# A streaming encoder step: the FFN up projection as seven block products for 768 of 1088 token columns

## The reference

```python
h = h + concat([conv_out, ret_out]) @ w_out
f = square(relu(rmsnorm(h, norm_ffn_w) @ w_up)) @ w_down     # w_up (1024, 4096), w_down (4096, 1024)
y = rmsnorm(h + f, norm_final_w)                             # 1024 prompt rows, 64 sample rows
```

## Time and profile before

| | |
|---|---|
| median of 3 runs | 1220.26 us (1220.0 to 1220.28) |
| profiled execution, first to last instruction (span) | 1218.5 us |
| granted TensorE clock | 1.000 of full speed, whole span |
| a middle group, up half | 23.76 us |
| the same group, down half | 20.90 us |

### The profile page before, as it was taken

One profiled execution on the slowest core, in us unless ns is written; L12 is line 12 of the kernel. 1 busy time (PEld: TensorE's weight loads), 2 busy tenths in 40 slices (PEclk: granted clock), 3 DMA queues, 4 the chain that ended last, 5 costly groups with the idle time before them and its releaser, 6 DMA issues.

```text
span 1218.5 us, 20456 instructions
## 1 busy us (share of the span) xinstructions
PE 1209.5 (99%) x6671; PEld 1119.4 (92%) x6671; DVE 763.3 (63%) x1483; ACT 524.4 (43%) x1154; POOL 290.9 (24%) x228
## 2 busy tenths in 40 slices
PE   8999999999999999999999999999999999999998
PEld 6899999999999888989989988998998998998996
DVE  5345665665666363477577568568568567666747
ACT  6414324333244342435434534544544533543546
POOL 0000000000000000252452452453353344345213
PEclk9999999999999999999999999999999999999999
DMA  7011111111111530121011111202201202102104
GB/s 265 22 35 40 40 46 37 48 37 37 51 42 63 180 106 1 52 70 61 25 53 60 46 31 60 67 10 60 69 9 60 69 9 69 60 9 69 52 18 148
DMA packets 84990, 69.52 MB, mean 57 GB/s; under 512 B 9416, under 2 KB 68816, under 8 KB 84960
## 3 DMA queue, kind: packets, MB, share of 16 engines
q1 hardware_dynamic: 84816, 68.89, 18.4%
q10 hardware_dynamic: 144, 0.26, 0.1%
HBM read 64.14 MB, written 4.99 MB: 57 GB/s over the span
## 4 chain that ended last, share of the span: by engine, by line
PE 98%; DMA 0%; ACT 0%; DVE 0%; SPq 0%; issue 0%; DVEq 0%; ACTq 0%
PE pp L1533 30%; PE pp L1535 30%; PE pp L1534 30%; PE pp L1539 1%; PE pp L1540 1%; PE pp L1730 1%; PE pp L1659 1%; PE pp L1670 1%; PE pp L1652 1%; PE pp L1669 1%; PE pp L1550 0%; DMA xr<-in_x_prompt 0%; PE pp L1641 0%; PE pp L1676 0%; SPq L474 0%; ACT junk L619 0%
## 5 line engine op out<-in xcount | busy, mean ns | idle before, releaser
L1535 PE MATMUL pp<-mid_hi,ws_lo 128*128 128x368 f32 (+1 forms) x768 | 251.4, 327 | 0.0
L1533 PE MATMUL pp<-mid_hi,ws_hi 128*128 128x368 f32 (+1 forms) x768 | 251.1, 327 | 0.0
L1534 PE MATMUL pp<-mid_lo,ws_hi 128*128 128x368 f32 (+1 forms) x768 | 250.8, 327 | 0.0
L1533 PE MATMUL pp<-hn_hi,ws_hi 128*128 128x368 f32 (+2 forms) x576 | 191.8, 333 | 0.0
L1341 DVE TENSOR_TENSOR h<-pp,h 128x512 f32<-128x512 f32 x300 | 190.3, 676 | 0.0
L1481 POOL TENSOR_TENSOR h<-tmp,h 128x512 f32<-128x512 f32 x120 | 158.4, 1352 | 131.6 <-ACT tmp L844 131.6
L1534 PE MATMUL pp<-hn_lo,ws_hi 128*128 128x368 f32 (+2 forms) x576 | 188.9, 328 | 0.0
L1535 PE MATMUL pp<-hn_hi,ws_lo 128*128 128x368 f32 (+2 forms) x576 | 188.8, 328 | 0.0
L1533 PE MATMUL pp<-do_hi,fo_hi 128*128 128x512 f32 x452 | 176.0, 389 | 0.0
L1534 PE MATMUL pp<-do_lo,fo_hi 128*128 128x512 f32 x452 | 175.9, 389 | 0.0
L1535 PE MATMUL pp<-do_hi,fo_lo 128*128 128x512 f32 x452 | 175.9, 389 | 0.0
(11 more groups left out here) (214 smaller groups left out, 1901.5 us busy)
## 6 DMA issues: line engine op xcount, KB each, us to landing
raw<-in_w_up SPq DMA_DIRECT2D x64, 256.0 KB, 4.8
dr<-in_w_down SPq DMA_DIRECT2D x64, 256.0 KB, 3.5
raw<-in_w_in SPq DMA_DIRECT2D x48, 256.0 KB, 2.9
xr<-in_x_prompt SPq DMA_DIRECT2D x8, 512.0 KB, 6.1
raw<-in_w_out SPq DMA_DIRECT2D x16, 256.0 KB, 3.3
out<-hw SPq DMA_DIRECT2D x9, 256.0 KB, 2.0
wv_raw<-in_w_in SPq DMA_DIRECT2D x8, 256.0 KB, 5.9
h<-in_x_prompt SPq DMA_DIRECT2D x2, 1024.0 KB, 7.9
```

Of the source, the lines that this page charges most:

```text
L1533: pe.matmul(out, a_hi, b_hi, start=start, stop=False, skip_group_check=again)
L1534: pe.matmul(out, a_hi, b_lo, start=False, stop=False, skip_group_check=again)
L1535: return pe.matmul(out, a_lo, b_hi, start=False, stop=stop, skip_group_check=again)
```

## The change

The up projection of token columns 0 to 767 becomes seven products as well. With the `w_up` slice of a group as four blocks A11, A12 (`a` = 0, contraction halves 0 and 1), A21, A22 (`a` = 1) and the tokens as blocks B11, B21 (columns 0 to 383) and B12, B22 (384 to 767):
- GpSimd combines the weights in each group: S3 = A11 - A21, S2 = A22 - S3, S4 = A12 - S2, S1 = A21 + A22.
- The combinations of the normed tokens (T1 to T4) are made once, by GpSimd beside the output projection, written to a device memory tensor `xt_dram` and read back; T1 goes over columns 384 to 767 of `mid`'s first contraction half, where B12 stood. B22 stays in the second half.
- TensorE's up half of groups 1 to 15 is D0, P1, P2, P6, P5, P7, P3, P4, D1. D0 and D1 are the direct products of the remaining 320 columns (256 prompt, 64 sample). P6, P7, P4 accumulate on P1 in bank 1; P3 on P5 in bank 2. Three intermediate results are copied out by ScalarE (`tap_copy`) for VectorE's sums (`c_sum`) before the bank goes on. Group 0 keeps the direct form for all columns (`up_first`), with parts of 384, 384 and 320.
- Weights, activations and their combinations share nine slots (`A_AT`, `W_AT`), and most raw data stands in place where its lo part is then written; `tmp`, `raw`, `dr` and the small sample tiles of the feed-forward part have no region of their own any more.
- The sample rows' relu and square move from ScalarE to VectorE (`sample_relu`). Their products move from the end of the down half to a place behind P1, into banks 4 and 5, which P2's third and fourth quarter use next.
- `OUT_TILES` becomes 0, 3, 1, 4, 8, 2, 5, 6, 7, and the pieces of `h` are waited for accordingly.

The core of the diff:

```diff
-CGY = [(0, 368), (368, 368), (736, 352)]
+SB = 384
+CGY = [(0, SB), (SB, SB), (2 * SB, TY - 2 * SB)]
+DIRECT = 2 * SB
...
+A_AT = {"A11": 0, "A21": 1, "A12": 2, "A22": 3, "S3": 4, "S2": 5, "S1": 6, "S4": 1}
+W_AT = {"A11": 0, "A12": 2, "S1": 3, "S3": 4, "S2": 5, "S4": 6, "A21": 7, "A22": 8}
+UPS = ["D0", "P1", "P2", "P6", "P5", "P7", "P3", "P4", "D1"]
+UP_BANK = {"D0": 0, "P1": 1, "P6": 1, "P7": 1, "P4": 1, "P2": 2, "P5": 2, "P3": 2, "D1": 3}
-ORDER = [*[(p, q) for p in range(OPS) for q in range(QUADS)], "sample"]
+ORDER = [*[(P1, q) for q in range(QUADS)], ("sample", 0), ("sample", 1), *[(p, q) for p in range(P2, OPS) for q in range(QUADS)]]
...
# ScalarE
+            def up_group(g):
+                w_hi_part(g, "S2")
+                w_hi_part(g, "S1")
+                f_direct(g, 0)
+                f_hi(g, "f1", F_HI)
+                d_hi_next(g, "B11")
+                tap_copy(g, "P1")
+                w_hi_part(g, "S3")
+                d_hi_next(g, "T1")
+                f_added(g, "C11")
+                w_hi_part(g, "S4")
+                tap_copy(g, "P6")
+                d_hi_next(g, "B21")
+                w_hi_part(g, "A22")
+                tap_copy(g, "P5")
+                d_hi_next(g, "T3")
+                w_hi_part(g, "A21")
+                f_added(g, "C22")
+                d_hi_next(g, "B22")
+                f_added(g, "C12")
+                f_hi(g, "A11", F_HI)
+                d_hi_next(g, "T2")
+                f_c21(g)
+                f_hi(g, "A12", F_HI)
+                d_hi_next(g, "T4")
+                f_direct(g, 1)
...
# VectorE
+            def up_group(g):
+                w_lo_part(g, "S2")
+                w_lo_part(g, "S1")
+                sample_relu(g, 0)
+                w_lo_part(g, "S3")
+                c_sum(g, "C11")
+                w_lo_part(g, "S4")
+                d_low(g, "B11", D_LO, D_HI)
+                d_low(g, "T1", D_LO, D_HI)
+                w_lo_part(g, "A22")
+                c_sum(g, "C22")
+                w_lo_part(g, "A21")
+                d_low(g, "B22", D_LO, D_HI)
+                c_sum(g, "C12")
+                d_low(g, "B21", D_LO, D_HI)
+                d_low(g, "T2", D_LO, D_HI)
+                d_low(g, "T3", D_LO, D_HI)
                 f_low(g, "A11", F_HI)
...
+                d_low(g, "T4", D_LO, D_HI)
+                f_low(g, "A12", F_HI)
+                sample_relu(g, 1)
+
+            def down_group(g, first):
+                dve.wait_ge(s_relu, 2 * g + 2)
+                dve.tensor_tensor(sf_raw(2), sf_raw(0), sf_raw(1), ALU.add).then_inc(f_sum_dve, 1)
+                dve.wait_ge(f_sum_dve, 3 * g + 1)
                 f_low(g, "f1", F_HI)
...
+                dve.tensor_tensor(fo_raw[:, A_AT["S2"], :], fr[:, 1, 512:1024], fo_raw[:, A_AT["S3"], :], ALU.add).then_inc(f_sum_dve, 1)
+                f_low(g, "f2", F_HI)
+                f_low(g, "f12", F_HI)
+                dve.tensor_tensor(fo_raw[:, A_AT["S1"], :], fr[:, 0, 512:1024], fr[:, 1, 512:1024], ALU.add).then_inc(f_sum_dve, 1)
                 add(g, P1, 0)
                 f_low(g, "S2", F_HI)
                 add(g, P1, 1)
                 add(g, P1, 2)
+                sample_add(g, 0)
+                add(g, P1, 3)
+                sample_add(g, 1)
...
                 add(g, P5, 3)
-                f_low(g, "f12", F_HI)
+                w_lo_part(g + 1, "A11")
+                add(g, P4, 0)
+                w_lo_part(g + 1, "A12")
+                add(g, P4, 1)
+                add(g, P4, 2)
                 add(g, P4, 3)
...
# GpSimd, in a group: T1 T3 T2 T4, then the activations' S3 and S4 (now in two steps), the adds of P6, then
+                pool.wait_ge(prod_done, NPROD * g + n_prod(P7, 3))
+                pool.tensor_tensor(s3, a11, a21, ALU.subtract).then_inc(ww_sum, 1)
...
+                pool.tensor_tensor(s2, a22, s3, ALU.subtract).then_inc(ww_sum, 1)
...
+                pool.tensor_tensor(s4, a12, s2, ALU.subtract).then_inc(ww_sum, 1)
+                pool.wait_ge(prod_done, NPROD * g + n_prod(P4, 3))
+                pool.tensor_tensor(s1, a21, a22, ALU.add).then_inc(ww_sum, 1)
+                for q in range(QUADS):
+                    add(g, P3, q)
...
# TensorE, in up_product: what a product waits for besides its operands
+                elif name == "P6":
+                    pe.wait_ge(tap_ready, 3 * (g - 1) + 1)
+                elif name == "P5":
+                    pe.wait_ge(c_add, 3 * (g - 1) + 1)
...
# TensorE, in product
+                    elif q >= 2:
+                        pe.wait_ge(samp_add, 2 * g + q - 1)
```

More of the change, by code:

```diff
@@ L93 @@
 BANK2 = [7, 3, 4, 5]
+SAMPLE_BANKS = [4, 5]
 IN_BANK1 = [P1, P6, P7, P4]
@@ L313, in build @@
         f_ready = sem("f_ready")
-        neg_ready = sem("neg_ready")
-        dr_in = [sem(f"dr_in{n}") for n in range(4)]
+        dr_in = {name: sem(f"dr_in_{name}") for name in ("B11", "B12", "B21", "B22")}
         d_sum = sem("d_sum")
@@ new lines, in _ @@
+            for name in ("A11", "A12", "A21", "A22"):
+                load_w(0, name, W_AT0[name])
+            for n in range(PAIRS):
+                sp.wait_ge(part_sum, n + 1)
+                for i in range(4):
+                    sp.dma_start(xt_dram[i, :, :, n * P:(n + 1) * P], parts[i].rearrange("p (k c) -> p k c", k=4)).then_inc(part_out, 16)
+            sp.wait_ge(ht_done, TILES)
+            for name in ("B11", "B12", "B22", "B21"):
+                load_d(0, name, do_hraw[:, P7, :] if name == "B12" else do_raw[:, D_OF[name], :])
@@ new lines, in xt_hi_part, with d_hi_next, up_first @@
+            def xt_hi_part(name):
+                act.wait_ge(xt_in[name], 16)
+                act.activation(xt_part(name, xt_hi, mid_hi), xt_part(name, xt_raw, mid_lo_raw), ACT.Copy).then_inc(xt_hi_ready, 1)
+            def d_hi_next(g, name):
+                q = {"B11": 0, "B21": 1, "T2": 2, "T1": 3, "B12": 2}.get(name)
+                if q is not None:
+                    act.wait_ge(pool_add, NCOPY * (g - 1) + n_pool(P3, q))
+                d_hi(g, name)
+            def up_first():
+                w_hi_part(0, "A21", True)
+                w_hi_part(0, "A22", True)
+                f_first(0, 0)
+                d_hi(0, "B11")
+                d_hi(0, "T1")
+                d_hi(0, "B21")
+                f_first(0, 1)
+                d_hi(0, "T3")
+                d_hi(0, "B22")
+                f_first(0, 2)
+                f_hi(0, "f1", F_HI)
+                d_hi(0, "T2")
+                d_hi(0, "T4")
+                f_first(1, 0)
+                f_hi(0, "A11", F_HI)
+                xt_hi_part("T2")
+                xt_hi_part("T3")
+                f_first(1, 1)
+                f_hi(0, "A12", F_HI)
+                f_first(1, 2)
@@ L1759, in _, with up_first @@
                         transposed(p - 1)
-            def up(g, first):
+            def up_first():
                 for a in range(2):
-                    order = [(half, j) for half in range(2) for j in UP_ORDER[a]]
-                    if first and a == 0:
+                    order = [(half, j) for half in range(2) for j in range(3)]
+                    if a == 0:
                         order = [(0, 0), (0, 1), (1, 0), (1, 1), (0, 2), (1, 2)]
@@ L1790, in up, with direct @@
                             last.then_inc(up_done, 1)
-                        elif j == UP_ORDER[a][2]:
-                            last.then_inc(w_used, 1)
+            def direct(g, a):
+                out = ps[UP_BANK[["D0", "D1"][a]]][:, 0:TY - DIRECT]
+                if a == 0:
+                    pe.wait_ge(dve_add, NDVE * (g - 1) + n_dve_add(P4, 0))
+                else:
+                    pe.wait_ge(act_copy, NCOPY * (g - 1) + n_copy(P3, 1))
+                for half in range(2):
+                    name = [["A11", "A12"], ["A21", "A22"]][a][half]
+                    pe.wait_ge(ww_ready, 8 * g + W_POS[name])
+                    for k in range(4):
+                        kk = 4 * half + k
+                        last = passes(out, w_part(fo_hi, W_AT[name], k), w_part(fo_lo, W_AT[name], k),
+                                      mid_hi[:, kk, DIRECT:TY], mid_lo[:, kk, DIRECT:TY], start=kk == 0, stop=kk == KT - 1)
+                last.then_inc(up_done, 1)
```

873 lines of the change are left out of this document (511 added, 362 removed).

## The result

The changed kernel takes 1271.3 us (1269.69 to 1272.88), before 1220.15 (1220.0 to 1220.28): ratio 1.0418, 95% interval [1.0403, 1.0433]. That is 51 us slower, on the side that was forecast, but 33 us above the forecast and outside its range.

What follows compares the result with a forecast made beforehand. PE's matmul start-to-start times were taken as the bound, VectorE close behind. Span 1218.5 - 32.1 (columns) + 44.8 (waits, 14 groups) + 5.5 (once only) + 1.8 (median above span) = 1238.5 us; range 1200 to 1256.

Steps and rivals of the forecast that it cites:

- The widths: Up half, groups 1 to 15: matmuls of 384 and 320 columns save 2.14 us per group, 32.1 us in all.
- Wait A: Down half, before P2's third and fourth product: PE waits for VectorE's sample adds to free the banks, 1.6 us per group.
- Wait B: Up half, before P6: PE waits for ScalarE's tap copy of P1, queued behind the f1 copy, 0.7 us per group.
- the restart: Late second matmul after a PE wait, named only after measuring; the prediction had no term for it.
- The exclusion: VectorE operations with both inputs in SBUF and GpSimd operations don't run together; a 64-column one took 1.00 us beside GpSimd.
- Wait C: Start of the down half: PE waits for VectorE's low split of A11, 0.9 us per group, 1.3 at most.
- The sample products: Down half, behind P1: f2 and f12 low parts ready at 2.7, PE asks at 2.73, so no wait counted.
- the waits feed each other: Slowest rival: a late tap delays the next copy, T1's and T3's splits slip; 4.7 us per group, 1259.5 us, chance 0.12.
- Once only: Losses outside the steady groups: group 0 1.6 and 1.4, group 1 1.8, group 15 0.7; together 5.5 us.
- queues keep clear: Faster rival: only the unavoidable 0.55 us of wait A remains in each of 15 groups; 1196.5 us, chance 0.27.

Runs made afterwards that it cites:

- the reordered kernel: Changed kernel with all queue moves, T2, T3, T4 split in the up half and group 0's x sum T4 split behind P7's adds; 1208.41 us, ratio 0.9902.
- A11's split first: Changed kernel with VectorE's split of A11 moved ahead of T2's and T3's in groups 1 to 14; 1275.18 us, ratio 1.0447.
- the tap copy first: Changed kernel with ScalarE's copy of sample part 1 (f1) moved from ahead of P1's tap copy to behind C11's square; 1261.89 us, ratio 1.0341.
- three moves: Changed kernel with sample adds earlier, P1's tap copy ahead of the f1 copy, and A11's split ahead of T2's and T3's; 1258.6 us, ratio 1.0319.
- the sample adds first: Changed kernel with VectorE's two sample adds moved ahead of S2's split and the adds of P1's third and fourth tile; 1250.84 us, ratio 1.0249.
- the shorter chain: Against three moves: f2 and f12 split before S2's sum, T2 behind A11, C11's sum before S3's split, T4 mid down half; 1245.68 us, ratio 1.0211.

## Why the prediction was wrong

Right: the side, and that PE's waits and not the columns decide. The widths gave what was said (pitches 173.8 and 146.3 ns for 173.5 and 146.8), no weight load held the 320s, no DMA ended a wait. The three waits stood where they were put, released as named, and VectorE's weight splits took 1098 ns in the mean, above the 949 named as a sign. The mechanism was right and its sizes were too small: the period was said to be 45.7 and is 47.40, and the time lies above even the slowest rival (1259.5). The steps of the sum that failed are these.

- *Wait A*, 1.6 said: 1.45. Another order took it away whole. GpSimd had a part in it too, since S2's split, which stood ahead of the sample adds, took 1.41 us beside GpSimd's last S4 step (at 627.54).
- *Wait B*, 0.7 said: 0.99, of which 0.11 is the restart, plus 0.19 before P5. The exclusion was named as the cause; half of wait B fell with GpSimd's adds.
- *Wait C*, 0.9 said: 1.76. This is the term of the sum that was most off, 12 of the 33 us. The order was as I had it: T2's and T3's splits, GpSimd's S4 step, A11's split:

```profile
620.17 1.32 DVE L1450 TENSOR_TENSOR do_lo<-do_raw,do_hi 128x512 fp32r<-128x512 f32 x2 [1.73 <-ACT do_hi L893]
621.41 1.76 DVE L1462 TENSOR_TENSOR fo_lo<-fo_flat,fo_hi 128x512 fp32r<-128x512 f32 x1
621.24 1.38 POOL L1719 TENSOR_TENSOR fo_hraw<-fo_flat 128x512 f32<-128x512 f32 x1 [0.90 <-ACT fo_flat L916]
```

  PE asked at 621.68 + 0.15 = 621.83, 7.68 us after P7's end as forecast. A11's split ended at 623.17, 9.02 us after it and not 8.6, since T2's and T3's splits ended 0.4 later than laid out and GpSimd's step began 0.2 later and took 1.38 us and not 1.15. PE began another 0.32 us after the split's end, and the restart took 0.10; these two were in no step. So 0.92 + 0.42 + 0.32 + 0.10 = 1.76. Why T2's copy on ScalarE, which VectorE waited for, was late is not shown.
- *The sample products*, nothing said ("2.7; PE's sample products ask at 2.73"): 0.40. The split of f12 ended 0.08 us after PE asked, and PE began 0.24 later still. Two ends 0.03 us apart should have been counted as a wait.
- *The restart* was not in the sum: 0.07 to 0.11 us behind each of six starts, some 0.6 us per group, 8 us in all. It is contained in the sizes given here.
- So a steady group lost 47.40 - 42.45 = 4.95 us and not 3.2, 69.3 us in 14 groups and not 44.8. The waits above are 4.8 of it; most of the rest is a pitch of 0.228 and not 0.227 us in the down half. The rival "the waits feed each other" had 4.7, but by another way (T1's and T3's splits late behind a late tap copy): its size was about met, and that way is not what the traces show.
- *Once only*, 5.5 said: 14.1. Group 0 lost 7.75, group 1 3.46 more than a steady one, the last up half 24.50 - (23.73 - 2.14) = 2.9. The step counted T4's and T1's x splits but not T2's and T3's, which stand before A12's; and in group 15 it did not see that ScalarE waits for all of GpSimd's adds ahead of D0's relu (a wait before P6 of 2.83, not 0.7). The slow matmuls (some twelve in group 0, nine in group 1) were in no step. Group 0's two x splits on VectorE, and ScalarE in group 15:

```profile
518.96 3.42 DVE L1496 TENSOR_TENSOR xt_lo<-xt_raw,xt_hi 128x1536 fp32r<-128x1536 f32 x2
...
1222.42 0.63 ACT L1035 ACTIVATE do_hraw<-h 64x512 f32<-64x512 f32 x1 [5.41 <-POOL h L1700]
```

- With these, 1218.5 - 32.1 + 69.3 + 14.1 = 1269.8 for a span of 1269.5.
- One side sum is off: a straight line between the sustained figures that the prediction takes from the Trainium skill gives 1.37 us per group and not 1.5, so 21 us and not 22 in 15 groups. Nothing else hangs on it.

What a sum of waits did not show is how they hang together. Two of them (C and the sample products) were one lateness of VectorE, since without the first the second grew from 0.40 to 2.35, and a third (A) covered the slow matmuls where the clock fell; what was worth removing could be seen only by moving things. The bound of "queues keep clear", 1196.5, was 12 us from what the reordered kernel takes.

Open: in the reordered kernel about 0.8 us per group, 6 us in group 0 and 1.3 in the last up half are still lost. Whether GpSimd's sums could be shortened, which would ease the same stretch, was not tried.

## What to carry to other kernels

When products are traded for sums on other engines, lay out the queue of the engine that does the sums from where its last slack ends, as one chain with all its users, and move out of it what no product needs yet. Bringing one operation forward gives nothing if all the others still stand ahead of the next user: A11's split first took 1.76 us from one place and added 1.95 at the next. Moving an operation back behind a user that does not need it gave the whole wait: S2's split behind the sample adds, 1.5 us per group. Order was worth more than any single cost here: the same 1656 VectorE operations made the kernel 51 us slower than before in one order and 12 us faster in another.

## What the runs showed of the hardware

- In the steady groups every wait of PE was followed by a late second matmul, 0.31 to 0.34 us after the first for 0.227 at 512 columns, 0.25 to 0.29 for 0.174 at 384. Wait A, which came in two parts, paid that twice.
- PE's clock fell to 1.2 GHz behind waits of 2.2 us and more in many cases and not in others of the same length: behind 2.2 us with the tap copy first in 6 of 13 groups, behind 2.3 us with A11's split first in 12 of the 13 groups 2 to 14, behind 2.6 us with three moves in 8 of 14; behind the same 2.83 us of group 15 not in the changed kernel but with the sample adds first; and not behind 3.35 us in group 0 of the shorter chain. Behind waits of 1.65 to 1.9 us, in some 80 groups of the runs, it never fell. A slow stretch was 7 to 12 matmuls of 512 columns at 0.43 us; 7 or 8 of them cost 1.6 us where nothing covers it.
- The VectorE operation with both inputs in SBUF and only 64 columns took 1.07 us beside GpSimd, 0.22 alone; GpSimd's adds of 16 columns took 0.3 us each, for 1.3 to 1.6 at 512.
